# Two hybrid blocks on one core: low parts of block 1's input weights by an accumulating transfer

## The chip, the cores and the metric

One core of one Trainium2 chip runs the whole program in one launch. The metric is the device time in microseconds (us), the median of several runs. All profiles here are of that one core.

## What is computed

Two models stand one behind the other, each with two layers on 512 tokens of width 1024. Block 1 prepends 16 meta tokens, so it works on T1 = 528 columns. A layer of it is, cut to what matters here:

```python
hn = rms_norm(h, norm_mix_g[l])
proj = hn @ w_in[l]                     # 1024 x 2560
q, k, v, xr, gate = jnp.split(proj, splits, axis=-1)
# q, k: rms_norm, partial rope, differential attention with v
# xr: causal conv, two gates, linear recurrence, times gelu(gate)
h = h + jnp.concatenate([o_attn, o_rec], axis=-1) @ w_out[l]
h = h + (silu(g) * u) @ w_down[l]       # g, u = rms_norm(h) @ w_gu[l]
```

Block 2 (another mixer, cross attention to a memory, a squared-relu MLP) follows; the change does not touch its work.

## The kernel before

**Products from two parts.** All large products run on TensorE (PE) in the fp32r format. Each fp32 weight and each activation is split into a high part (the value rounded to fp32r) and a low part (the rest), and a product is three passes: high x high (L589), low weight x high activation (L592), high weight x low activation (L595). `dense` issues these for one 128x128 tile of weights and 528 columns in two halves of 264; `token_major` (L684, L686, L688) does the same for the value projection `w_v`.

**Pieces.** Weights come in pieces of 128 x 1024 fp32 (512 KB), in one long order over the whole program. In each layer of block 1 the order is 4 pieces of `w_v`, 16 pieces of `w_in` (k, q, xr and gate tiles), 8 of `w_out`, then the feed-forward. SyncE's queue (SP) loads piece n into one of 3 staging buffers (`load`, L2654). ScalarE (ACT) copies it to the high half of one of 3 `weights_hi_lo` buffers (`split_hi`, L1196) once TensorE has finished piece n-3. VectorE (DVE) subtracts the high part from the staged weights and writes the low half (`split_lo`, L1766). SP may refill a staging buffer when both have read it.

**Steps of block 1's attention stage.** Every engine runs the same 80 steps, written out by hand, each in its own program order. Four steps are one tile of `w_in`: step s works on tile t = s // 4 with two of its eight 128-row chunks. Tiles alternate between two PSUM slots, and VectorE evicts a tile at s % 4 == 3 (L2013). ScalarE splits the high part of tile t+2 at the end of its step s = 4t, VectorE the low part near the end of its step 4t+1. So 14 of the 16 pieces are split inside steps 0, 4, ..., 52; the first two are split before the steps, behind the third and fourth piece of `w_v`. Between the tiles' products the steps hold small work that goes from engine to engine: attention units at fixed steps (PE scores L778 and L782, DVE maxima L1907 to L1910, ACT exponentials L1278, DVE reciprocals L1888, POOL scaling L2534, DVE combination L1991, PE transposes L848 and L851, ACT copies L1332 to L1338, PE weighted sums L860 and L864), norms of q and k and the rope (PE sums L661, DVE L1915, ACT L1238, L1240 and L1286, DVE L1787 to L1789, L1921, L1926), and the gates of the recurrence (DVE convolution L1934, PE L661, ACT tanh L1300, ACT L1306 to L1310, POOL L2547 to L2554, DVE scan L1949). Step 2 of layer 0 has a chain of small VectorE instructions (L1816 to L1845) that begins with two small ScalarE exponentials (L1433, L1435). ScalarE loads a table (1.28 us) whenever the function changes to one of another table.

**Queues.** POOL (GpSimd) issues no transfer in the kernel before: loads and stores go by SP's queue, a few by ScalarE's. Waits are on semaphores, and every engine works through its own queue in order.

Durations of single instructions stand in the rows below. The lines that the diff touches are in `split_hi`, `split_lo`, `pool_attention`, `sync_program`'s `load`, and `Kernel.low`:

```python
w.wait_ge(*K.done("hi", n))                                  # split_lo, VectorE
e.tensor_tensor(lo[:, 0:cols], K.staged(n)[:, 0:cols], hi[:, 0:cols].bitcast(F32), ALU.subtract)
```

Of the kernel before, what the change touches and what calls it, by code (L numbers as in the profile page):

```python
# [12 lines left out]
ALU = mybir.AluOpType  # L13
ACT = mybir.ActivationFunctionType
# [5 lines left out]
DEPTH = 2  # L20
# [38 lines left out]
STAGING, PARTS, TEMPS = 3, 3, 16  # L59
# [2 lines left out]
WARM = 16  # L62

LINE = 1024 // 4
LINE_PAD = 32
ACT_COLS = -(-DC * T1 // LINE) * LINE


# [15 lines left out]
def columns(params):  # L84
# [25 lines left out]
    root_act=("qk_root_act", "sub_root_act", "rec_root_act", "ln_root_act"),  # L110
    var=("qk_var", "sub_var", "rec_var", "ln_var"), square=("qk_square", "sub_square", "rec_square", "ln_square"),
    norm_stat=("qk_stat", "sub_stat", "rec_stat", "sq_stat", "mean_sum", "shift_sum"),
    hid_hi=("hid_hi2", "gx_hi", "gx_columns_hi"), hid_lo=("hid_lo2", "gx_lo", "gx_columns_lo"),
).items() for name in names}


class Tally:
# [14 lines left out]
    def did(self, name, *key, by=1):  # L132
        sem = SEM_OF.get(name, name)
        self.value[sem] = self.value.get(sem, 0) + by
        if self.sems is None:
            assert (name, key) not in self.at, (name, key)
        self.at[name, key] = self.value[sem]
        return self.sem(name), by

    def done(self, name, *key):  # L140
        return self.sem(name), self.at[name, key] if self.sems is not None else 0
# [17 lines left out]
class Counted:  # L159
# [5 lines left out]
    def wait_ge(self, sem, value):  # L165
        return self

    def dma_start(self, out, src):
        return self

    def matmul(self, out, weights, moving, start=True, stop=True):
# [55 lines left out]
def along(row, width):  # L227
    if width <= BANK:
# [6 lines left out]
ORDER1 = [("xr", 0), ("k", 0), ("q", 0), ("k", 1), ("xr", 1), ("q", 1), ("k", 2), ("q", 2), ("xr", 2), ("g", 0),  # L235
          ("k", 3), ("q", 3), ("xr", 3), ("g", 1), ("g", 2), ("g", 3)]
AT1 = {tile: n for n, tile in enumerate(ORDER1)}
W_IN = {"q": 0, "k": HEADS, "xr": 2 * HEADS, "g": 3 * HEADS}
# [67 lines left out]
PIECES = pieces()  # L306
PIECE = {key: n for n, key in enumerate(PIECES)}
# [91 lines left out]


POOL_SPLIT = {s: 4 + (s - TOK_STEPS) // 4 + 2 for s in range(IDX_STEP + 9, MEM_STEP, 8)}
POOL_PIECES = {PIECE["w_tok", _l, 0] + ahead for _l in range(DEPTH) for ahead in POOL_SPLIT.values()}


class Kernel:
# [57 lines left out]
        return ap[:, 0, :], ap[:, 1, :]  # L463

    def low(self, n):
        return self.done("lo_pool" if n in POOL_PIECES else "lo", n)

    def piece(self, n):
        name, *at = PIECES[n]
        ap = self.t[name]  # L470
        if name in ("w_down", "w_ff2"):
            l, m, k0, k1 = at
            return ap[l, m, :, k0 * P:k1 * P]
        return ap[tuple(at)]
# [715 lines left out]
def split_hi(e, w, K, n):  # L1190
    if n < len(PIECES):
        w.wait_ge(*K.done(LANDED[n % STAGING], n))
        if n >= PARTS:
            w.wait_ge(*K.done("product", n - PARTS))
        cols = K.piece(n).shape[-1]
        e.activation(K.parts(n)[0][:, 0:cols], K.staged(n)[:, 0:cols], ACT.Copy).then_inc(*K.did("hi", n))  # L1196


def scalar_start(e, w, K):
# [43 lines left out]
def scalar_attention(e, w, K, l):  # L1243
    m, did, done = K.m, K.did, K.done
    first = PIECE["w_v", l, 0]
    for p in range(3):
        split_hi(e, w, K, first + p + 3)
# [510 lines left out]
        scalar_block2(e, w, K, l)  # L1758


def split_lo(e, w, K, n, name="lo"):
    if n < len(PIECES):
        cols = K.piece(n).shape[-1]
        hi, lo = K.parts(n)
        w.wait_ge(*K.done("hi", n))
        e.tensor_tensor(lo[:, 0:cols], K.staged(n)[:, 0:cols], hi[:, 0:cols].bitcast(F32), ALU.subtract).then_inc(  # L1766
            *K.did(name, n))
# [371 lines left out]
def vector_mixers(e, w, K, l):  # L2139
# [4 lines left out]
    for s in range(TOK_STEPS, STEPS2 + 2):  # L2144
# [89 lines left out]
        if s == MEM_STEP:  # L2234
            for n in range(DC // 2):
# [3 lines left out]
                                ALU.subtract).then_inc(*did("in_lo", "mem", l, n))  # L2239
        if s % 4 == 1 and TOK_STEPS + 4 < s <= MEM_STEP + 1 and s not in POOL_SPLIT:  # L2240
            split_lo(e, w, K, first + 4 + (s - TOK_STEPS) // 4 + 2)
# [4 lines left out]
def vector_normed(e, w, K, l, name, key, alpha, early=False):  # L2246
# [57 lines left out]
    for n in range(half + 1):  # L2304
        low(n)
# [207 lines left out]
def square_sums(e, w, K, stage, l, width):  # L2513

    total = K.xc[:, 0:width]
    for k in range(1, DC):
        w.wait_ge(*K.done("square", stage, l, k))
        if k > 1:
            w.wait_ge(*K.done("square_sum", stage, l, k - 1))
        square = K.g1 if k == DC - 1 else K.sq1[k % 3]  # L2520
        e.tensor_tensor(total, total, square[:, 0:width], ALU.add).then_inc(*K.did("square_sum", stage, l, k))  # L2521


def pool_attention(e, w, K, l):
    m, did, done = K.m, K.did, K.done
    w.wait_ge(*done("landed_rope"))
    for s in range(STEPS1):
        if s - 2 in UNIT_AT1[l]:
            u, h, i = UNIT_AT1[l][s - 2]
            q0, rows, keys, whole = unit1(i)  # L2530
            b = K.probs1[u % 2][1][0:rows, 0:keys]
            w.wait_ge(*done("rates", l, u))
            w.wait_ge(*done("small", l, "done"))
            e.tensor_scalar(b, b, m["small"][u % 4][0:rows, 7:8], m["lam"][0:rows, l, 5:6], ALU.mult, ALU.mult).then_inc(  # L2534
                *did("scaled1", l, u))
        if s - 3 in STAT_AT1:
            kind, n = STAT_AT1[s - 3]
            dst = (K.k if kind == "k" else K.q)[:, n, :]
            w.wait_ge(*done("normed", l, kind, n))
            e.tensor_tensor(dst, K.raw1[kind == "q"], m["rope"][:, 0, :], ALU.mult).then_inc(*did("cos", l, kind, n))  # L2540
        for n in range(REC_TILES):
            r = GATE1[n, 0]
            if s == r + 1:
                half_rate = m["lsig"][:, l, n:n + 1]
                w.wait_ge(*done("gate_tanh", l, n, 0))
                w.wait_ge(*done("small", l, "done"))
                e.tensor_scalar(K.tr, K.tr, half_rate, half_rate, ALU.mult, ALU.add).then_inc(*did("rate", l, n))  # L2547
            if s == r + 3:
                w.wait_ge(*done("half_tanh", l, n))
                e.tensor_scalar(K.tr, K.tr, 0.0, None, ALU.max).then_inc(*did("max", l, n))  # L2550
            if s == r + 5:
                w.wait_ge(*done("mult_first", l, n))
                w.wait_ge(*done("gated_in", l, n))
                e.tensor_tensor(K.xc, K.xc, K.tr, ALU.mult).then_inc(*did("scan_in", l, n))  # L2554
        if s == SUBROOT[1] + 3:
            mixed1_lo(e, w, K, l, 1, K.q[:, 1, :], "in_lo_pool")
        if s - 1 in RECSQ:
            n = RECSQ.index(s - 1)
            if 0 < n < REC_TILES - 1:
                w.wait_ge(*done("rec_square", l, n))  # L2560
                if n > 1:
                    w.wait_ge(*done("rec_sums", l, n - 1))
                e.tensor_tensor(K.xc, K.xc, (K.xc, K.tr, K.ti)[n], ALU.add).then_inc(*did("rec_sums", l, n))
    square_sums(e, w, K, "f", l, T1 if l + 1 < DEPTH else T2)


def pool_mixers(e, w, K, l):
    m, did, done = K.m, K.did, K.done
    for s in range(TOK_STEPS, STEPS2):
        if s - 2 in UNIT_AT2:  # L2570
# [3 lines left out]
            e.tensor_scalar(prob, prob, m["small"][u % 4][:, 7:8], None, ALU.mult).then_inc(*did("scaled", l, u, 1))  # L2574
        if s in POOL_SPLIT:
            split_lo(e, w, K, PIECE["w_tok", l, 0] + POOL_SPLIT[s], "lo_pool")
        if s in ROT_AT2:
# [67 lines left out]
def sync_program(e, K):  # L2645
    w = Waits(e)
    m, t, did, done = K.m, K.t, K.did, K.done

    def load(n):
        if n >= STAGING:  # L2650
            w.wait_ge(*done("hi", n - STAGING))
            w.wait_ge(*K.low(n - STAGING))
        src = K.piece(n)
        e.dma_start(K.staged(n)[:, 0:src.shape[-1]], src).then_inc(*did(LANDED[n % STAGING], n, by=16))  # L2654

    for c in range(DC):
        e.dma_start(m["x"][:, c, META:T1], t["x_t"][:, c]).then_inc(*did(f"landed_x{c}", by=16))
        if c in (0, 2, 4):
            load(c // 2)
    e.dma_start(K.lams[:, 0:DEPTH * 4 * HEAD_DIM], t["lambdas"]).then_inc(*did("landed_lams", by=16))  # L2660
    e.dma_start(m["consts"][:, :], t["consts"][:, 0:C_CAUSAL]).then_inc(*did("landed_consts", by=16))
    e.dma_start(K.gates, t["w_gates"][0]).then_inc(*did("landed_gates", 0, by=16))
    e.dma_start(m["rope"][:, 0:2, :], t["consts"][:, C_COS1:C_COLS].rearrange("p (a n) -> p a n", a=2)).then_inc(
        *did("landed_rope", by=16))
    e.dma_start(K.once[:, 0:2 * P], t["consts"][:, C_CAUSAL:C_COS1]).then_inc(*did("landed_once", by=16))
    e.dma_start(m["par2"][:, :, :], t["params2"]).then_inc(*did("landed_params2", by=16))
    for n in range(STAGING, len(PIECES)):
        load(n)
    for c in range(DC):
        w.wait_ge(*done("ln_out", "w_ff2", DEPTH - 1, c))  # L2670
        e.dma_start(K.out[:, c, :], m["x"][:, c, META:T1]).then_inc(*did("stored", c, by=16))
    w.wait_ge(*K.last("stored"))
# [6 lines left out]
def build(nc, t, out):  # L2679
    with ExitStack() as ctx:  # L2680
        def sb(name, cols, dt=F32):
            return ctx.enter_context(nc.sbuf_tensor(name, [P] + list(cols), dt))

        sb("to_line", [LINE_PAD])
        m = dict(
# [197 lines left out]
```

## Time and profile before

| | us |
|---|---|
| median of 3 runs | 2858.15 |
| lowest and highest run | 2857.96, 2858.54 |
| span of the profiled execution | 2853.0 |
| busy in it: PE, weight loads of PE | 2772.6, 2353.1 |
| busy in it: DVE, ACT, POOL | 1639.5, 1267.9, 403.3 |

The span is counted from the first to the last instruction of the profiled execution; no separate whole time is given for that execution. The median of the runs is 5.15 us above the span, which is start and end around the instructions. "Busy" of PE counts overlapped matmuls with modelled ends, so short waits below some 0.2 us are hidden in it; the row of the weight load (PEld) beside a matmul then still shows them. In the rows, "<-" behind a time names what ended the idle time of the engine before that instruction.

### The profile page before, as it was taken

How to read it: one execution, taken by the hardware profiler on the slowest of the kernel's cores; microseconds unless marked ns; L12 is line 12 of the kernel's file. 1: busy time of each engine (PE TensorE's matmuls, PEld its weight loads, DVE VectorE, ACT ScalarE, POOL GpSimd, SP SyncE). 2: the span in 40 equal slices, each digit the busy share in tenths (PEclk: the TensorE clock that was granted, in tenths of full speed). 3: DMA queues.
4: the chain of work that ended last, by engine and by line, in shares of the span. 5: the costliest groups of instructions: out<-in, count | busy, mean ns of one | idle time of the engine just before them, and what ended most of it. 6: DMA issues, size and time to landing. Idle time of an engine off the chain costs nothing.

```text
span 2853.0 us, 39111 instructions
## 1 busy us (share of the span) xinstructions
PE 2772.6 (97%) x15784; PEld 2353.1 (82%) x15784; DVE 1639.5 (57%) x2465; ACT 1267.9 (44%) x2133; POOL 403.3 (14%) x305
## 2 busy tenths in 40 slices
PE   9999999999989999999999999999999999999997
PEld 8878999999877788887668888888776688888886
DVE  6776545454777745454876466333658764753335
ACT  5674322224674422233564545333445644443333
POOL 2222000001222000001333120000313331200003
PEclk9999999999999999999999999999999999999999
DMA  4112232232112233332123223333222232233322
GB/s 153 45 45 67 89 97 85 94 92 83 49 45 74 93 96 97 102 93 89 56 75 126 88 67 96 98 95 96 85 82 63 75 126 81 67 104 96 96 96 67
DMA packets 71923, 244.35 MB, mean 86 GB/s; under 512 B 9153, under 2 KB 10817, under 8 KB 71745
## 3 DMA queue, kind: packets, MB, share of 16 engines
q1 hardware_dynamic: 67392, 237.28, 26.4%
q10 hardware_dynamic: 4352, 4.58, 0.5%
q8 instruction: 126, 2.06, 0.3%
q14 instruction: 53, 0.43, 0.0%
HBM read 239.73 MB, written 2.10 MB: 85 GB/s over the span
## 4 chain that ended last, share of the span: by engine, by line
PE 86%; DVE 8%; ACT 4%; issue 2%; POOL 0%; DMA 0%; ACTq 0%; DVEq 0%; SPq 0%
PE psum L589 24%; PE psum L595 24%; PE psum L592 24%; PE psum L661 2%; PE psum L684 1%; PE psum L688 1%; PE psum L686 1%; PE psum L922 1%; PE psum L1095 1%; PE psum L1107 1%; PE psum L950 1%; PE psum L939 1%; PE psum L975 1%; DVE weights_hi_lo L1766 1%; PE psum L778 1%
## 5 line engine op out<-in xcount | busy, mean ns | idle before, releaser
L589 PE MATMUL psum<-act_hi_lo,weights_hi_lo 128*128 128x264 f32 (+2 forms) x2544 | 777.6, 345 | 3.7 <-ACT temp L1300 2.8
L592 PE MATMUL psum<-act_hi_lo,weights_hi_lo 128*128 128x264 f32 (+2 forms) x2544 | 752.2, 335 | 1.9 <-DVE weights_hi_lo L1766 1.9
L595 PE MATMUL psum<-act_hi_lo,weights_hi_lo 128*128 128x264 f32 (+2 forms) x2544 | 753.4, 335 | 0.0
L1196 ACT ACTIVATE weights_hi_lo<-weights_float 128x1024 fp32r<-128x1024 f32 (+2 forms) x446 | 463.6, 1042 | 499.8 <-PE psum L595 430.6
L1766 DVE TENSOR_TENSOR weights_hi_lo<-weights_float,weights_hi_lo 128x1024 fp32r<-128x1024 f32 (+2 forms) x432 | 540.7, 1252 | 219.0 <-ACT weights_hi_lo L1196 217.8
L589 PE MATMUL psum<-hidden_hi_lo,weights_hi_lo 128*128 128x512 f32 (+2 forms) x1584 | 520.2, 358 | 3.7 <-DVE x_residual L2020 1.4
L595 PE MATMUL psum<-hidden_hi_lo,weights_hi_lo 128*128 128x512 f32 (+2 forms) x1584 | 512.2, 353 | 1.4 <-DVE hidden_hi_lo L2030 1.4
L592 PE MATMUL psum<-hidden_hi_lo,weights_hi_lo 128*128 128x512 f32 (+2 forms) x1584 | 511.8, 353 | 1.3 <-DVE weights_hi_lo L1766 1.3
L589 PEld LDWEIGHTS psum<-act_hi_lo,weights_hi_lo 128*128 128x128 f32 x2544 | 440.5, 189 | 68.1 <-issue 17.7
L595 PEld LDWEIGHTS psum<-act_hi_lo,weights_hi_lo 128*128 128x128 f32 x2544 | 439.3, 189 | 47.9
L592 PEld LDWEIGHTS psum<-act_hi_lo,weights_hi_lo 128*128 128x128 f32 x2544 | 438.7, 189 | 47.7 <-issue 2.6
L589 PEld LDWEIGHTS psum<-hidden_hi_lo,weights_hi_lo 128*128 128x128 f32 x1584 | 280.1, 189 | 44.9 <-DVE x_residual L2020 2.0
L595 PEld LDWEIGHTS psum<-hidden_hi_lo,weights_hi_lo 128*128 128x128 f32 x1584 | 279.8, 189 | 42.3 <-DVE hidden_hi_lo L2030 2.0
L592 PEld LDWEIGHTS psum<-hidden_hi_lo,weights_hi_lo 128*128 128x128 f32 x1584 | 279.7, 189 | 40.4 <-DVE weights_hi_lo L1766 1.7
L2036 DVE SCALAR_TENSOR_TENSOR x_residual<-x_residual,psum 128x512 f32<-128x512 f32 (+1 forms) x108 | 74.7, 691 | 275.2 <-PE psum L595 275.2
L2436 DVE TENSOR_TENSOR hidden_hi_lo<-temp,hidden_hi_lo 128x512 fp32r<-128x512 f32 x52 | 36.0, 692 | 172.2 <-ACT hidden_hi_lo L1697 172.2
L1409 ACT ACTIVATE hidden_hi_lo<-temp 128x528 fp32r<-128x528 f32 (+1 forms) x44 | 28.1, 639 | 201.8 <-DVE temp L2072 201.8
L2605 POOL TENSOR_TENSOR act_hi_lo<-x_residual 128x512 fp32r<-128x512 f32 x4 | 8.9, 2221 | 736.7 <-DVE x_residual L2036 736.7
L2521 POOL TENSOR_TENSOR temp<-temp 128x528 f32<-128x528 f32 (+1 forms) x28 | 43.6, 1558 | 479.7 <-ACT temp L1232 479.0
L1726 ACT ACTIVATE temp<-psum 128x512 f32<-128x512 f32 x52 | 31.1, 598 | 136.5 <-PE psum L595 136.5
L1404 ACT ACTIVATE temp<-temp 128x528 f32<-128x528 f32 (+1 forms) x44 | 28.1, 639 | 132.9 <-DVE temp L2060 132.8
L2574 POOL TENSOR_SCALAR temp<-temp,small 128x512 f32<-128x512 f32 (+3 forms) x48 | 54.8, 1143 | 186.3 <-DVE small L2157 186.1
(294 smaller groups left out, 3343.0 us busy)
## 6 DMA issues: line engine op xcount, KB each, us to landing
weights_float<-in_w_ff SPq DMA_DIRECT2D x128, 512.0 KB, 3.6
weights_float<-in_w_gu SPq DMA_DIRECT2D x88, 512.0 KB, 3.6
weights_float<-in_w_in SPq DMA_DIRECT2D x70, 512.0 KB, 3.7
weights_float<-in_w_down SPq DMA_DIRECT2D x32, 448.0 KB, 3.3
weights_float<-in_w_out SPq DMA_DIRECT2D x16, 512.0 KB, 3.6
weights_float<-in_w_down SPq DMA_DIRECT2D x16, 512.0 KB, 3.5
weights_float<-in_w_mv SPq DMA_DIRECT2D x16, 512.0 KB, 3.3
weights_float<-in_w_mix SPq DMA_DIRECT2D x16, 512.0 KB, 3.5
```

The costliest lines, as they stand in the source:

```text
L589: e.matmul(slot[:, place:place + c1 - c0], w_hi[:, col], x_hi[:, c0:c1], start=first, stop=False)
L592: e.matmul(slot[:, place:place + c1 - c0], w_lo[:, col], x_hi[:, c0:c1], start=False, stop=False)
L595: mm = e.matmul(slot[:, place:place + c1 - c0], w_hi[:, col], x_lo[:, c0:c1], start=False, stop=final)
L661: mm = e.matmul(slot[:, place:place + c1 - c0], weights, moving[:, c0:c1], start=first, stop=final)
L684: e.matmul(bank, act[:, 0, here], w_hi[:, wk], start=k == 0, stop=False)
L1196: e.activation(K.parts(n)[0][:, 0:cols], K.staged(n)[:, 0:cols], ACT.Copy).then_inc(*K.did("hi", n))
L1726: e.activation(raised(f), K.bank[2 * RING["w_ff1", l, f]], ACT.Relu).then_inc(*did("relu", l, f))
L1766: e.tensor_tensor(lo[:, 0:cols], K.staged(n)[:, 0:cols], hi[:, 0:cols].bitcast(F32), ALU.subtract).then_inc(*K.did(name, n))
L2036: e.scalar_tensor_tensor(along(x, width), along(x, width), alpha, across(K.psum[slot], width), ALU.mult, ALU.add).then_inc(*K.did(*mark))
L2436: e.tensor_tensor(lo, raised(f), hi.bitcast(F32), ALU.subtract).then_inc(*did("hid_lo2", l, f))
L2521: e.tensor_tensor(total, total, square[:, 0:width], ALU.add).then_inc(*K.did("square_sum", stage, l, k))
L2574: e.tensor_scalar(prob, prob, m["small"][u % 4][:, 7:8], None, ALU.mult).then_inc(*did("scaled", l, u, 1))
```

## The change

For the 16 pieces of `w_in` of each of block 1's two layers (32 pieces in all) ScalarE writes, right after the high part, the negated weights in fp32r, which is the negated high part, into the low half of the buffer. POOL's queue then issues a transfer of the same piece from memory with the operation "add" onto that low half, which leaves weights minus high part there. VectorE's subtraction of these pieces is gone, and TensorE waits for the transfer in its place. SP waits for the negation in place of the low part before it refills a staging buffer. POOL issues the first two transfers before its step 0 and the others at the end of its steps 1, 5, ..., 53. Some semaphores are shared by names that one engine signals in order, a scratch area for POOL's transfers grows from 256 to 1024 bytes, and a padding tensor grows with it so that later tensors keep their place within a line.

```diff
 LINE = 1024 // 4
-LINE_PAD = 32
+LINE_PAD = 96
@@
+    bias=("far", "near"), lam_exp=("lsig_exp",), mean=("mean_square",), conv_first=("conv2_first",), cube=("gelu_tanh",),
+    hi=("negated",),
@@
+SUM_PIECES = {PIECE["w_in", _l, _n] for _l in range(DEPTH) for _n in range(16)}
+SUM_LOW = [f"lo_sum{n}" for n in range(PARTS)]
@@
     def low(self, n):
+        if n in SUM_PIECES:
+            return self.done(SUM_LOW[n % PARTS], n)
         return self.done("lo_pool" if n in POOL_PIECES else "lo", n)
+
+    def read(self, n):
+        return self.done("negated", n) if n in SUM_PIECES else self.low(n)
@@ split_hi
         e.activation(K.parts(n)[0][:, 0:cols], K.staged(n)[:, 0:cols], ACT.Copy).then_inc(*K.did("hi", n))
+        if n in SUM_PIECES:
+            e.activation(K.parts(n)[1][:, 0:cols], K.staged(n)[:, 0:cols], ACT.Copy, scale=-1.0).then_inc(*K.did("negated", n))
@@
+def add_low(e, w, K, n):
+    w.wait_ge(*K.done("negated", n))
+    e.dma_start(K.parts(n)[1], K.piece(n), accum_op=ALU.add).then_inc(*K.did(SUM_LOW[n % PARTS], n, by=16))
@@ split_lo
-    if n < len(PIECES):
+    if n < len(PIECES) and n not in SUM_PIECES:
@@ pool_attention
+    first = PIECE["w_in", l, W_IN[ORDER1[0][0]] + ORDER1[0][1]]
     w.wait_ge(*done("landed_rope"))
+    for p in range(2):
+        add_low(e, w, K, first + p)
     for s in range(STEPS1):
...
+        if s % 4 == 1 and s // 4 + 2 < len(ORDER1):
+            add_low(e, w, K, first + s // 4 + 2)
@@ load
-            w.wait_ge(*K.low(n - STAGING))
+            w.wait_ge(*K.read(n - STAGING))
@@ kernel
-    nc = bacc.Bacc("TRN2", ..., dynamic_dma_scratch_size=256)
+    nc = bacc.Bacc("TRN2", ..., dynamic_dma_scratch_size=1024)
```

## Rows read from the trace of the kernel before

**Rows 1.** The page: busy us, share of the span and instructions of each engine.

```profile
PE 2772.6 (97%) x15784; PEld 2353.1 (82%) x15784; DVE 1639.5 (57%) x2465; ACT 1267.9 (44%) x2133; POOL 403.3 (14%) x305
```

**Rows 2.** Windows: stretch, length, busy PE, PEld, DVE, ACT, POOL; clock, DMA share, GB/s.

```profile
35.00:175.00 140.00, 129.73 (x941) 115.92 (x940) 101.28 (x179) 90.46 (x161) 32.59 (x29) 0.99 0.16 50
...
250.00:640.00 390.00, 389.11 (x3190) 388.58 (x3189) 193.21 (x253) 106.45 (x133) 10.85 (x7) 1.00 0.29 90
...
690.00:830.00 140.00, 128.45 (x954) 116.01 (x952) 99.92 (x151) 91.83 (x156) 32.23 (x29) 1.00 0.16 50
```

**Rows 3.** Waits of PE, 35 to 185 us: us in total, times, longest.

```profile
PE psum L778 <- ACT arena L1278: 2.4, 2, 1.7
PE psum L778 <- DVE arena L2013: 1.6, 1, 1.6
PE psum L661 <- ACT temp L1286: 1.5, 2, 0.8
PE psum L851 <- DVE arena L1991: 1.2, 1, 1.2
```

**Rows 4.** Lines L1766 and L1196 in layer 0's steps: ns min/median/max.

```profile
L1766 DVE TENSOR_TENSOR weights_hi_lo<-weights_float,weights_hi_lo x14: 1201/1218/1226, 38.7 to 183.9; 128x1024 fp32r<-128x1024 f32 x14
...
L1196 ACT ACTIVATE weights_hi_lo<-weights_float x14: 1039/1044/1063, 37.5 to 180.1; 128x1024 fp32r<-128x1024 f32 x14
```

**Rows 5.** Timeline, layer 0 from step 0: start, us, engine, [idle before <- releaser].

```profile
37.51 1.06 ACT L1196 ACTIVATE weights_hi_lo<-weights_float 128x1024 fp32r<-128x1024 f32 x1 [2.06 <-PE psum L688]
...
40.12 0.16 DVE L1816 TENSOR_TENSOR lambdas<-lambdas 128x1 f32<-128x1 f32 x1 [0.22 <-ACT lambdas L1433]
...
48.85 0.19 PEld L661 LDWEIGHTS psum<-temp,arena 128*128 128x128 f32 x1 [0.27 <-issue]
```

**Rows 6.** Timeline, layer 1 at step 20 to 22.

```profile
733.73 1.04 ACT L1196 ACTIVATE weights_hi_lo<-weights_float 128x1024 fp32r<-128x1024 f32 x1
...
736.78 0.69 ACT L1278 ACTIVATE arena<-psum,small 128x528 f32<-128x528 f32 x1
...
737.61 0.52 PEld L661 LDWEIGHTS psum<-temp,consts 128*128 128x128 f32 x3 [0.20 <-ACT arena L1278]
```

**Rows 7.** Timeline, layer 0 behind step 28, and layer 1's counterpart.

```profile
104.72 1.05 ACT L1196 ACTIVATE weights_hi_lo<-weights_float 128x1024 fp32r<-128x1024 f32 x1
...
113.42 0.46 PE L860 MATMUL psum<-temp,arena 128*128 128x128 f32 x2 [0.16 <-ACT temp L1338]
...
763.40 0.39 ACT L1338 ACTIVATE temp<-psum 128x256 f32<-128x256 f32 x1 [0.30 <-PE psum L851]
```

**Rows 8.** Timeline, layer 0 behind steps 40 and 44.

```profile
143.53 1.04 ACT L1196 ACTIVATE weights_hi_lo<-weights_float 128x1024 fp32r<-128x1024 f32 x1
...
146.63 1.16 PE L661 MATMUL psum<-temp,arena 128*128 128x264 f32 x4 [1.05 <-ACT temp L1300]
...
154.24 1.04 ACT L1196 ACTIVATE weights_hi_lo<-weights_float 128x1024 fp32r<-128x1024 f32 x1
...
156.52 1.26 PE L778 MATMUL psum<-arena 64*128 64x512 f32 x8 [0.76 <-ACT arena L1278]
```

**Rows 9.** Timeline, layer 0: ACT behind the split of step 36.

```profile
134.07 0.49 ACT L1338 ACTIVATE arena<-psum 128x384 f32<-128x384 f32 x1 [2.29 <-PE psum L851]
```

**Rows 10.** The page: DMA queue 1, and issues of `w_in` pieces with us to landing.

```profile
q1 hardware_dynamic: 67392, 237.28, 26.4%
...
weights_float<-in_w_in SPq DMA_DIRECT2D x70, 512.0 KB, 3.7
```

**Rows 11.** Timeline: layer 1's splits of `w_in` 0 and 2, and SP's `w_in` loads.

```profile
675.10 1.06 ACT L1196 ACTIVATE weights_hi_lo<-weights_float 128x1024 fp32r<-128x1024 f32 x1 [5.86 <-PE psum L688]
...
689.82 1.06 ACT L1196 ACTIVATE weights_hi_lo<-weights_float 128x1024 fp32r<-128x1024 f32 x1 [2.06 <-PE psum L688]
...
12.75 134.97 SPq L2654 DMA_DIRECT2D weights_float<-in_w_in  x16
```

**Rows 12.** Timeline, POOL behind step 29 in layer 0.

```profile
108.70 0.46 POOL L2534 TENSOR_SCALAR arena<-arena,small,lambdas 128x144 f32<-128x144 f32 x1 [3.74 <-DVE small L1888]
```

More of the change, by code:

```diff
@@ L166, in wait_ge, with dma_start @@
         return self
-    def dma_start(self, out, src):
+    def dma_start(self, out, src, accum_op=None):
         return self
@@ L2872 @@
     arrays = layout({name: np.asarray(a) for name, a in inputs.items()})
-    nc = bacc.Bacc("TRN2", target_bir_lowering=False, num_devices=1, dynamic_dma_scratch_size=256)
+    nc = bacc.Bacc("TRN2", target_bir_lowering=False, num_devices=1, dynamic_dma_scratch_size=1024)
     feed, aps = {}, {}
```

## The prediction

> **What bounds the kernel.** I read the page's busy times first: PE is busy 2772.6 of 2853.0 us [rows 1], so all other engines together can give back at most 80.4 us, and only where PE waits. The windows say where that is. In the feed-forward stretch from 250 to 640 us PE lacks 0.9 us of 390. In the steps of block 1's attention it lacks 140 - 129.73 = 10.3 us in layer 0 and 140 - 128.45 = 11.5 us in layer 1, with VectorE busy 72% and ScalarE 65% [rows 2]. These are the stretches in which the 32 pieces are split. No engine is full there; what counts is which wait of PE ends last, and on whom. The waits say that ScalarE releases as many of them as VectorE: exponentials and squares against evictions and combinations [rows 3], and the gate tanh [rows 8]. Nobody waits there for the subtraction itself. So the question of this change is not how much work VectorE loses, but in which uninterrupted queue run of which engine the removed and the added instruction stand when PE is waiting for something behind them.
>
> **Removed: VectorE's subtraction.** 32 x 1.22 us [rows 4] = 39 us of VectorE time. It is worth something only where PE's releaser stands behind it in one run without idle time. I followed each of PE's waits back. The eviction (1.6 us) [rows 3] and the norms' waits hang on runs of VectorE that begin, behind the subtraction, with idle time that PE or ScalarE ends. L1926 at steps 33 and 53 follows the subtraction without a gap, but PE's rope product ends within 0.05 us of its start. The combinations (L1991) wait for POOL or for a ScalarE root. I find no wait of PE with a subtraction in the run ahead of it, so I take 0; the bounds are 0 and, if every wait on VectorE shrank, what rival C prices.
>
> **Added: ScalarE's negation.** The same form as the high copy, so 1.04 us each [rows 4], 32 x 1.04 = 33 us of ScalarE time. Most of it falls into idle time: behind step 36 for example ScalarE next sat idle 2.29 us until PE [rows 9]. Where a releaser of PE stands in the same run behind the copy, PE starts 1.04 us later, and as PE is the full engine nothing later takes that back. The places, each read off the timeline:
> - Layer 0, step 0: the copy at 37.51 us is followed by the small exponentials that start VectorE's small chain, on which VectorE sat idle 0.22 us. The chain delays the first eviction, the convolution and so the first gate product, whose weight load at 48.85 us had already waited 0.27 us [rows 5]: 1.04. Layer 1 has no such chain.
> - Step 20, both layers: the copy, a table load and two exponentials follow without a gap; the second ends 0.14 us before PE's rope sum, which had waited for it 0.20 us [rows 6]: 2 x 1.04.
> - Step 28, layer 0: a full run from 104.72 us to the copy of turned probabilities, for which PE waited at 113.42 us: 1.04. In layer 1 the same copy had been idle 0.30 us and PE came 1.3 us later [rows 7]: 0.
> - Step 40, both layers: the gate tanh right behind the copy, for which PE already waits 1.05 us: 2 x 1.04.
> - Step 44, both layers: the exponentials right behind the copy, for which PE waits 0.76 us at 156.52 us [rows 8]: 2 x 1.04. The wait after it hangs on the same run and is no second loss.
> Together 8 x 1.04 = 8.3 us. The other 20 negations in the steps and the four before them I cost at nothing: the idle time of ScalarE behind them hides them, and if it were gone each would cost up to 1.04 us more. That is the upper bound of this term, 33 us; the lower one is 0.
>
> **Moved: who makes the low part.** PE's wait moves from VectorE to a transfer that POOL issues. The tightest piece is `w_in` 0: its high copy starts at 675.10 us in layer 1 and its product when `w_v` 3 ends, just before 689.82 us [rows 11]. Copy and negation take 2.1, which leaves 12.6 us; the later tiles leave about as much or more, since they are two tiles ahead too. No row shows an accumulating transfer. The nearest is the plain load of the same bytes, 3.7 us to landing; all of queue 1's packets took 26.4% of 2853 us for 237.28 MB, which is 1.7 us for 0.52 MB [rows 10]. The other end is a transfer several times as slow, which I put at 20 us, above all that the windows allow. I take one whose moving part doubles: 3.7 + 1.7 = 5.4 us, well inside 12.6, so 0 for PE. The Trainium skill says in "Collectives: The Full Stack" (The bandwidth ceiling) that a reduce runs at about half the rate of a copy because the add needs two source reads; by it the landing would be this same 5.4 us, and no run here shows it yet.
>
> POOL: 16 issues a layer behind its steps' work. Each wait for a negation stands ahead of POOL's next step. The tightest of these places is behind step 29: the next instruction comes at 108.70 us after 3.74 us idle, of which the negation (to 106.8) leaves 1.9 [rows 12]. I take up to 1.9 us for one on POOL and so 0; with 4 us it would push L2534 and a combination at two or three steps a layer, some 1 us each, 2 to 6 in all. The memory traffic rises by 32 x 0.52 = 16.8 MB, in stretches that move 50 GB/s [rows 2]: 0. SP's refill condition comes earlier, and no load is waited for: 0. The shared semaphores keep the order of one engine: 0. The larger scratch and pad keep the tensors' places: 0.
>
> **Sum.** The profiled execution had a span of 2853.0 us, 5.15 below the median of the runs. 2853.0 + 8.3 = 2861.3 us of span, and 2858.15 + 8.3 = **2866.5 us**. A measurement of this kernel tells about 0.2%, 5.7 us, from no change.
>
> **The rivals.**
> - A, the delay is absorbed: PE's later waits shrink by what the earlier ones lost, because some releasers run on their own clock (a combination of VectorE that waits for POOL). Then half or less remains, 0 to 5.7 us: about 2861. For it: rows 3 has such a wait of 1.2 us. Against it: nearly every run of ScalarE and VectorE here begins with a release by PE.
> - B, the transfer is late. It decides from a landing of 12.6 us. A pair of tiles takes 2 x 135 / 15 = 18 us [rows 11], and copy, negation and landing must fit in it: at 20 us landing each pair is 4.1 us too long, 7 pairs in 2 layers, +57 us, 2915; at 14 to 16 us only the first, shorter tiles stall, +10 to +20. Against it: the plain load has three times the room that it needs. For it: POOL's path and the add are not in the trace. The Trainium skill warns in "SBUF — State Buffer" (SBUF: two separate sides) that VectorE's two-port operations lock GpSimd out while it writes descriptors, and gives 620 ns that became 3100. By that ratio a plain landing of 3.7 would be 18.5 us, on this rival's side; it needs such an operation standing over each issue, and the VectorE rows here are mostly two-input operations and copies of 0.3 us. I give the lock 0.04 of this rival's 0.15.
> - C, faster: VectorE's queue, 0.9 of its 1.2 us shorter each tile, reaches PE through evictions and combinations, and ScalarE's negation disappears in idle time. PE's two largest groups of waits on VectorE in layer 0 are 1.6 and 1.2 us [rows 3]; twice that for layer 1 is 5.6, and with the smaller waits I estimate at most 10: 2848. It decides if subtractions do stand in the runs that release PE; I found none.
> - D, the low part is made as said but costs POOL 4 us an issue: +2 to +6 on top, 2870. It lies inside my range.
>
> **How the numbers follow.** The forecast, alone or with D: 0.56; A: 0.21; B: 0.15; C: 0.08. Below 2852.4 us is only C: 0.08. Within 0.2% are A and the low edge of the forecast (five or fewer of the eight places hold): 0.21 + 0.03 = 0.24. Slower are the rest of the forecast and B: 0.68. The range takes in A almost whole from 2859.5 us and goes up through D, up to half of the unseen extra places, and B's mild part, to 2884 us; it leaves out C, A's edge and B's late end.
>
> **What would show it.** ScalarE's busy time +33 us and VectorE's -39; PE's idle time in the two stretches up by 5.2 in layer 0 and 3.1 in layer 1. The wait at 146.6 us becomes 2.1 us, the one at 156.5 us 1.8, and the rope sum behind step 20 shows a wait of 1.2 us on L1278. PE's waits on the transfer are nil, and its landing is under 12 us. I am wrong if PE's L592 waits for the transfer, if POOL's issue takes over 2 us and L1991's waits grow, or if those five places show no longer waits.

## The result, and the profile after

The changed kernel takes 2863.85 us (median of 10 runs, 2862.35 to 2867.32), the kernel before on the same chip 2857.37 us (10 runs, 2856.12 to 2859.88). The ratio is 1.0025, 95% interval 1.0016 to 1.0034: slower by 7.1 us (4.6 to 9.7). The forecast was slower by 8.3 us, 2866.5 us, with a range of 2859.5 to 2884.

Busy times, queues and transfers on the page of the changed kernel (to be set against [rows 1], [rows 4] and [rows 10]; a DMA line ends with KB each and the us from issue to landing):

```profile
PE 2778.2 (97%) x15784; PEld 2356.6 (82%) x15784; DVE 1602.7 (56%) x2433; ACT 1298.3 (45%) x2165; POOL 428.9 (15%) x337
...
q1 hardware_dynamic: 67392, 237.28, 25.9%
q0 software_dynamic: 4608, 16.78, 3.5%
...
weights_float<-in_w_in SPq DMA_DIRECT2D x70, 512.0 KB, 3.8
weights_hi_lo<-in_w_in POOLq DMA_DIRECT2D x32, 512.0 KB, 7.9
```

VectorE lost 36.8 us of work, ScalarE gained 30.4, POOL 25.6, and 16.78 MB of transfers came on. The span rose by 8.6 us, to 2861.6. None of the work that moved has that size; the waits of PE tell where the time went.

The timeline of the changed kernel at the places named in the prediction (start us, duration us, engine, line; L1205 is the high copy, L1207 the negation, L670 and L787 are PE's L661 and L778 of before). First steps 0, 20 and 28 of layer 0:

```profile
38.01 1.06 ACT L1205 ACTIVATE weights_hi_lo<-weights_float 128x1024 fp32r<-128x1024 f32 x1 [2.06 <-PE psum L697]
38.98 1.04 ACT L1207 ACTIVATE weights_hi_lo<-weights_float 128x1024 fp32r<-128x1024 f32 x1
...
50.40 0.46 PE L670 MATMUL psum<-temp,arena 128*128 128x264 f32 x1 [1.10 <-issue]
...
88.09 1.16 PE L670 MATMUL psum<-temp,consts 128*128 128x264 f32 x4 [0.94 <-ACT arena L1289]
...
110.11 0.22 PE L787 MATMUL psum<-arena 64*16 64x16 f32 x4 [0.27 <-ACT arena L1289]
...
116.88 0.46 PE L869 MATMUL psum<-temp,arena 128*128 128x128 f32 x2 [0.76 <-ACT temp L1349]
...
121.66 0.18 PE L860 MATMUL psum<-consts,arena 16*16 16x16 f32 x1 [0.59 <-DVE arena L2009]
```

Then steps 40 and 44, in layer 0 and (from 804 us) in layer 1, where the kernel before waited 1.52 and 1.19 us, as the second block shows:

```profile
146.39 1.04 ACT L1205 ACTIVATE weights_hi_lo<-weights_float 128x1024 fp32r<-128x1024 f32 x1
147.34 1.04 ACT L1207 ACTIVATE weights_hi_lo<-weights_float 128x1024 fp32r<-128x1024 f32 x1
...
150.45 1.16 PE L670 MATMUL psum<-temp,arena 128*128 128x264 f32 x4 [1.99 <-ACT temp L1311]
...
161.28 1.26 PE L787 MATMUL psum<-arena 64*128 64x512 f32 x8 [1.71 <-ACT arena L1289]
...
804.71 1.69 PE L670 MATMUL psum<-temp,arena 128*128 128x264 f32 x3 [2.47 <-ACT temp L1311]
...
816.31 1.26 PE L787 MATMUL psum<-arena 64*128 64x512 f32 x8 [1.94 <-ACT arena L1289]
```

```profile
797.88 1.16 PE L661 MATMUL psum<-temp,arena 128*128 128x264 f32 x4 [1.52 <-ACT temp L1300]
...
807.57 1.26 PE L778 MATMUL psum<-arena 64*128 64x512 f32 x8 [1.19 <-ACT arena L1278]
```

What the reader is to see: in layer 0 the copy and the negation each last 1.04 us, but start 0.95 apart, so a negation delays what is behind it by 0.95. The waits of 1.05 and 0.76 us [rows 8] became 1.99 and 1.71; the rope sum behind step 20, whose weight load had waited 0.20 (layer 1's is in [rows 6], layer 0's is as long), waits 0.94; the 0.16 at step 28 [rows 7] is 0.76, with 0.27 ahead of it.

I laid the same instructions of both traces beside each other and read how far PE's start had moved. The kernel with the negation on VectorE (run e7 below) serves as the reference: its median is that of the kernel before, and it has no half-clock stretch (one in which PE's granted clock is 0.5, 1.2 GHz) near 164 us, which before has. The move grows by 1.01 at step 0, 0.95 at step 20, 0.34 and 0.59 at step 28, falls by 0.61 right behind it, where PE's wait for a combination shrank (above: 0.59 us at 121.66 us, 1.19 before), and grows by 0.93 at step 40 and 0.94 at step 44. That is +4.2 us for layer 0. In layer 1 half-clock stretches lie near the same places in this pair of profiles (3.4 us each from 739.4, 804.2 and 817.9 us in the changed kernel's), so single steps can't all be read off there. The traces of e9 (below) and of before have no such stretch at these three places: set beside each other, PE's start moves by 0.95, 0.93 and 0.95 at steps 20, 40 and 44. That is 2.8 us, and a gate product ahead of them, behind a gate tanh of ScalarE, adds 0.3 (also in e3, below, and not in e2). Sum: 7.3 us, against the ratio's 7.1.

### The profile page after: what moved, and what is told of

The parts are those of the page before. It is cut to its first block, busy times and chain, and to the rows that moved or that the text cites. A ratio compares the mean times of both kernels' runs of the same rounds, so it can differ in the third digit from the quotient of the medians.

```text
span 2861.6 us, 39138 instructions
## 1 busy us (share of the span) xinstructions
PE 2778.2 (97%) x15784; PEld 2356.6 (82%) x15784; DVE 1602.7 (56%) x2433; ACT 1298.3 (45%) x2165; POOL 428.9 (15%) x337
## 3 DMA queue, kind: packets, MB, share of 16 engines
q0 software_dynamic: 4608, 16.78, 3.5%
## 4 chain that ended last, share of the span: by engine, by line
PE 85%; DVE 9%; ACT 4%; issue 2%; POOL 0%; DMA 0%; ACTq 0%; DVEq 0%; SPq 0%
PE psum L598 24%; PE psum L601 23%; PE psum L604 23%; PE psum L670 2%; PE psum L693 1%; PE psum L697 1%; PE psum L695 1%; PE psum L931 1%; PE psum L1104 1%; PE psum L1116 1%; PE psum L959 1%; PE psum L948 1%; PE psum L984 1%; ACT weights_hi_lo L1205 1%; DVE weights_hi_lo L1784 1%
## 5 line engine op out<-in xcount | busy, mean ns | idle before, releaser
L1205 ACT ACTIVATE weights_hi_lo<-weights_float 128x1024 fp32r<-128x1024 f32 (+2 forms) x446 | 463.7, 1042 | 498.7 <-PE psum L604 431.0
L1784 DVE TENSOR_TENSOR weights_hi_lo<-weights_float,weights_hi_lo 128x1024 fp32r<-128x1024 f32 (+2 forms) x400 | 501.6, 1255 | 201.5 <-ACT weights_hi_lo L1205 200.2
L2605 POOL TENSOR_TENSOR arena<-temp,rope_tables 128x512 f32<-128x512 f32 x14 | 18.1, 1291 | 441.2 <-ACT temp L1488 441.2
```

## Experiments

The ratio is that of each kernel to the kernel before on the same chip; "us" is (ratio - 1) x 2857. Kernels whose computation differs: e2, whose transfers add the weights to what the low half held.

| run | what is different | ratio (95%) | us |
|---|---|---|---|
| the change | | 1.0025 (1.0016 to 1.0034) | +7.1 |
| e1 | negations without the transfers | 1.0020 (1.0010 to 1.0029) | +5.7 |
| e2 | transfers without the negations | 1.0001 (0.9993 to 1.0010) | +0.3 |
| e3 | 24 pieces, without the eight places | 0.9996 (0.9987 to 1.0004) | -1.1 |
| e4 | the eight places alone | 1.0023 (1.0014 to 1.0032) | +6.6 |
| e5 | 29 pieces, five negations moved | 0.9998 (0.9989 to 1.0006) | -0.6 |
| e6, e11 | before, three splits a layer moved | 0.9996 (0.9987 to 1.0005), 0.9994 (0.9985 to 1.0003) | -1.1, -1.7 |
| e7 | VectorE negates | 1.0001 (0.9992 to 1.0010) | +0.3 |
| e8 | transfers two steps later | 1.0024 (1.0016 to 1.0033) | +6.9 |
| e9 | transfers four steps later | 1.0036 (1.0021 to 1.0051) | +10.3 |
| e10 | every negation twice | 1.0094 (1.0079 to 1.0110) | +26.9 |
| e12 | e6 with one subtraction later | 0.9991 (0.9982 to 1.0000) | -2.6 |

### Which part costs: e1 and e2

```diff
 split_lo (e1; the transfers are gone)
-    if n < len(PIECES) and n not in SUM_PIECES:
+    if n < len(PIECES):
...
-        w.wait_ge(*K.done("hi", n))
+        w.wait_ge(*K.done("negated" if n in SUM_PIECES else "hi", n))
```

> The changed kernel with the transfers taken out: ScalarE's 32 negations stay, and VectorE subtracts as before, over them. Theory S (the whole cost is ScalarE's negation in eight places, 0.95 us each as the profile after shows, 7.6 in all, less 0.6 absorbed): +7 us against the kernel before, about 2864.5 where that one has 2857.4, and the waits of 1.7 to 2.0 us at 150 and 161 us. Theory T (the transfers or POOL's issues cost it): 0, waits of 0.8 and 1.0 there. Theory V (the removed subtractions give back some us, and the negations cost more than 7): +10 or more.

```diff
 read, split_hi, add_low (e2)
-        return self.done("negated", n) if n in SUM_PIECES else self.low(n)
+        return self.done("hi", n) if n in SUM_PIECES else self.low(n)
...
-        if n in SUM_PIECES:
-            e.activation(K.parts(n)[1][:, 0:cols], K.staged(n)[:, 0:cols], ACT.Copy, scale=-1.0).then_inc(*K.did("negated", n))
...
-    w.wait_ge(*K.done("negated", n))
+    w.wait_ge(*K.done("hi", n))
```

> The changed kernel without ScalarE's negations: POOL's transfer adds the weights to what the low half held, as soon as the high copy is there, so the low parts of these 32 pieces have wrong values; VectorE's subtractions are gone. Theory S: 0 us against before (2857.4), within 1.5. Theory T: +7. Theory V: -3 or less. Landing 7.9 us and POOL's issue 0.9 us as in the profile after, in every theory.

e1 has nearly the whole cost (+5.7), e2 none (+0.3). e2 by itself shows a sum: 32 subtractions fewer and 32 transfers more come to nothing, within 2.9 us. That neither hides the other is told by the waits: those of PE for VectorE from 35 to 190 us are in e2 what they are in before (1.6, 1.2, 0.9, 0.5 and 0.4 us), and there is none for a transfer. So the subtractions are worth nothing, and the transfers cost nothing. e1's waits are those of the whole change. Its waits of PE from 35 to 190 us (us in total, times, longest), and under them e2's:

```profile
PE psum L785 <- ACT arena L1287: 3.7, 3, 1.7
PE psum L668 <- ACT temp L1309: 2.0, 1, 2.0
...
PE psum L668 <- issue: 1.0, 1, 1.0
PE psum L668 <- ACT arena L1287: 0.9, 1, 0.9
```

```profile
PE psum L670 <- ACT temp L1309: 1.1, 1, 1.1
...
PE psum L670 <- issue: 0.2, 1, 0.2
```

In e2 the step-40 wait is 1.1 again, and of the waits at steps 0 and 20 only 0.2 us are left ("issue"). Its profiled span was 2859.4 us, though: that execution took 2861.24 us, the longest of its eleven, 5.1 above their median. The waits of one profile say more here than its length.

### Which places: e3 and e4

```diff
-SUM_PIECES = {PIECE["w_in", _l, _n] for _l in range(DEPTH) for _n in range(16)}
+AT_STEPS = [{0, 20, 28, 40, 44}, {20, 40, 44}]
+SUM_PIECES = {PIECE["w_in", _l, 0 + W_IN[ORDER1[_s // 4 + 2][0]] + ORDER1[_s // 4 + 2][1]]
+              for _l in range(DEPTH) for _s in range(-8, 56, 4) if _s not in AT_STEPS[_l]}   # e3
+              for _l in range(DEPTH) for _s in AT_STEPS[_l]}                                 # e4
...
 add_low
+    if n not in SUM_PIECES:
+        return
```

> The change for 24 of the 32 pieces: the eight whose negation stands ahead of a releaser of PE (layer 0: steps 0, 20, 28, 40, 44; layer 1: steps 20, 40, 44) are split as before. Theory S: 0 to +0.5 us against before (0.2 to 0.3 for a gate tanh behind a table load in layer 1). Theory T: 24/32 of the cost, +5. A theory that the delay is spread over all negations: +5 as well.

> The change for those eight pieces alone. Theory S: +6.5 to +7.6 us against before, nearly all of what the whole change costs. Theory T and the theory of a spread delay: 8/32 of it, +2.

24 of the 32 pieces change nothing that can be told (-1.1 us, interval -3.7 to +1.1), eight pieces make nearly all of it (+6.6). The busy times do not show this: e3 gave ScalarE three quarters of the added work. The busy times on e3's page, then on e4's:

```profile
PE 2772.5 (97%) x15784; PEld 2350.8 (82%) x15784; DVE 1611.0 (56%) x2441; ACT 1289.9 (45%) x2157; POOL 422.4 (15%) x329
```

```profile
PE 2777.6 (97%) x15784; PEld 2356.2 (82%) x15784; DVE 1630.9 (57%) x2457; ACT 1275.6 (45%) x2141; POOL 409.0 (14%) x313
```

ScalarE is busier by 22 us in e3 (span 2851.7) and by 8 us in e4 (span 2861.1).

### The same work in another place: e5 and e7

```diff
+MOVED = [{0: 1, 20: 22, 40: 43}, {20: 22, 40: 43}]        # e5; steps 28 (layer 0) and 44 split as before
...
 scalar_attention, end of step s
+        for step, at in MOVED[l].items():
+            if s == at:
+                negate(e, w, K, first + 4 + step // 4 + 2)
```

> The change for 29 of the 32 pieces, with five negations moved off the places that release PE: that of step 0 in layer 0 behind the small exponentials, that of step 20 to the end of step 22 and that of step 40 to the end of step 43 in both layers, where ScalarE sat idle. The pieces of step 28 in layer 0 and of step 44 in both layers are split as before. Theory S (a negation costs by its place): 0 against the kernel before, within 1 us. Theory T (transfers or POOL cost): +6. A theory that the number of negations counts: 29/32 of the change's cost, +6. A late landing (negation of step 40 ends about 10 us ahead of its tile, landing 7.9): PE waits of under 1 us at L601 of the changed kernel.

```diff
 split_lo on VectorE (e7), in place of ScalarE's L1207
-    if n < len(PIECES) and n not in SUM_PIECES:
+    if n in SUM_PIECES:
+        w.wait_ge(*K.done("hi", n))
+        e.tensor_scalar(K.parts(n)[1], K.staged(n)[:, :], -1.0, None, ALU.mult).then_inc(*K.did("negated", n))
+    elif n < len(PIECES):
...
```

> The change with the negation on VectorE, where the subtraction stood, and not on ScalarE. Theory S: 0 against the kernel before, within 1.5 us, since no wait of PE stands behind that place of VectorE's queue, and ScalarE works as before. Theory T: +7. The negation takes 0.6 to 1.2 us on VectorE.

Both are at zero. e5's timeline at step 20: the exponentials come first, and the negation at 85.29 us stands in idle time of ScalarE; at step 40 the wait is 1.05 us, as before:

```profile
85.20 0.20 ACT L1297 ACTIVATION_READ_ACCUMULATOR arena<-psum,small 128x1 f32 x1
85.29 1.05 ACT L1215 ACTIVATE weights_hi_lo<-weights_float 128x1024 fp32r<-128x1024 f32 x1
...
85.46 1.16 PE L674 MATMUL psum<-temp,consts 128*128 128x264 f32 x4
...
146.51 1.16 PE L674 MATMUL psum<-temp,arena 128*128 128x264 f32 x4 [1.05 <-ACT temp L1319]
```

e7's lines for the subtraction that is left and for the negation (duration in ns, least, median, most):

```profile
L1784 DVE TENSOR_TENSOR weights_hi_lo<-weights_float,weights_hi_lo x400: 1091/1225/2367, 7.4 to 2820.4; 128x1024 fp32r<-128x1024 f32 x121, 128x896 fp32r<-128x896 f32 x11, 128x912 fp32r<-128x912 f32 x2
L1779 DVE TENSOR_SCALAR weights_hi_lo<-weights_float x32: 671/685/694, 26.8 to 833.7; 128x1024 fp32r<-128x1024 f32 x32
```

VectorE negates in 0.69 us what ScalarE negates in 1.04, in a place that no wait of PE hangs on: PE's waits from 35 to 190 us are those of before. It is the version to choose if the transfers are wanted, and it wins nothing either.

### The room of the transfer: e8 and e9

```diff
-        if s % 4 == 1 and s // 4 + 2 < len(ORDER1):
-            add_low(e, w, K, first + s // 4 + 2)
+        if s % 4 == 3 and s // 4 + 2 < len(ORDER1):               # e8
+            add_low(e, w, K, first + s // 4 + 2)
+        if s % 4 == 1 and s >= 4 and s // 4 + 1 < len(ORDER1):    # e9
+            add_low(e, w, K, first + s // 4 + 1)
```

> The changed kernel with POOL's transfers of the steps issued two steps later (about 4.5 us). My account (landing 7.9 us, and 8 steps of 2.2 to 3.2 us from a copy to its tile, less four for issue): they land 0 to 2 us ahead of their tiles, PE waits for them under 1 us in all, and the time is that of the changed kernel, +7 against before. If the landing is less even than its 5.8 to 8.4 us, or POOL comes late behind its own waits: L601 of PE waits for transfers, +10 to +20.

> The changed kernel with POOL's transfers of the steps issued four steps later, at the end of the second step of the tile ahead. What is left to a landing of 5.7 to 7.9 us is then about the 2.7 steps to the tile, 6 us and more where a step has other work. My account: PE now waits for transfers in about half of its 28 tiles, 1 to 4 us each, the time rises by 20 to 80 us over the changed kernel, and L601 and its weight load show it: so the room is real, and between two and four steps of delay it ends. If the transfer had more room than I worked out: no wait, +7 against before as with two steps.

e8 costs nothing more (+6.9 against +7.1), and PE waits for no transfer. In e9 it does. Two waits of layer 0 in its timeline, and from the view of the transfer's line who waited for it in the whole run (us, times):

```profile
64.56 0.51 PE L601 MATMUL psum<-act_hi_lo,weights_hi_lo 128*128 128x264 f32 x2 [3.14 <-DMA weights_hi_lo<-in_w_in]
...
73.10 0.51 PE L601 MATMUL psum<-act_hi_lo,weights_hi_lo 128*128 128x264 f32 x2 [0.65 <-DMA weights_hi_lo<-in_w_in]
```

```profile
  PE psum L601: 9.0, 7
```

So the room ends between two and four steps, as worked out, but my size for it was wrong: seven waits and not half of 28, 9.0 us of waiting, and the medians are 3.2 us apart, against the 20 to 80 I expected. (e9 has three executions, and the profiled one is the longest of them, 3.8 us above their median, so the 9.0 and the 3.2 are not of one execution.) The two longest waits, 3.14 us here and 3.12 in layer 1, are early, where a step holds little besides the tile; in the later, longer steps most transfers had landed. Part of this waiting comes back: up to the eviction wait at 83.87 us the two waits shown, 3.8 us, move PE by 1.7 us only, since four waits behind them shrink, those of 0.70, 0.44 and 0.78 us to nothing and that of 1.58 [rows 3] to 1.34. So a delay of PE by a transfer is in part taken back here, which the delay of ScalarE at the eight places is not: the waits that shrink are those for squares of ScalarE and for VectorE's statistics and eviction, which these two waits of PE held up less than PE itself.

### More of it: e10

```diff
-    hi=("negated",),
+    hi=("negated", "negated_once"),
...
         if n in SUM_PIECES:
+            e.activation(K.parts(n)[1][:, 0:cols], K.staged(n)[:, 0:cols], ACT.Copy, scale=-1.0).then_inc(*K.did("negated_once", n))
+            w.wait_ge(*K.done("negated_once", n))
             e.activation(K.parts(n)[1][:, 0:cols], K.staged(n)[:, 0:cols], ACT.Copy, scale=-1.0).then_inc(*K.did("negated", n))
```

> The changed kernel with every negation done twice, the second after the first: ScalarE gets another 1.0 to 1.1 us at each place. Theory S: the same places pay again, 8 x 1.05 = 8.4 us, and some of the others join, since their idle time behind the negation is used up: +8 to +14 over the changed kernel, +15 to +21 against before. A theory of a fixed cost of the change (transfers, POOL's issues): +7 against before, as with one.

The second negation costs 19.8 us more, nearly three times the first, and above the range I had given. The old places paid another 1.1 each (3.08 us at step 40, 1.99 with one negation), and places whose cover one negation had just used up began to pay:

```profile
67.24 1.13 PE L670 MATMUL psum<-temp,consts 128*128 128x264 f32 x4 [1.69 <-ACT temp L1299]
...
107.80 1.16 PE L670 MATMUL psum<-temp,arena 128*128 128x264 f32 x4 [0.76 <-ACT temp L1313]
...
143.01 1.16 PE L670 MATMUL psum<-temp,consts 128*128 128x264 f32 x4 [0.73 <-ACT arena L1291]
...
159.13 1.27 PE L670 MATMUL psum<-temp,arena 128*128 128x264 f32 x4 [3.08 <-ACT temp L1313]
```

The first of these is one of two waits on the square behind an eviction: 1.5 us together before and with one negation [rows 3], 2.5 with two. The cost of one more microsecond on ScalarE is convex: all but zero in 24 places, but by little in many of them.

### A version that uses the reading: e6, e11, e12

If a negation costs 0.95 us in a place, the high copy that stands there already costs as much, as far as PE's wait reaches. e6 is the kernel before, with no part of the change, and three splits a layer moved:

```diff
+SPLIT_AT = {20: 22, 40: 43, 44: 47}
 scalar_attention; vector_attention the same with SPLIT_AT.get(step, step) + 1 and split_lo
-        if s % 4 == 0 and s < 4 * len(ORDER1):
-            split_hi(e, w, K, first + 4 + s // 4 + 2)
+        for step in range(0, 4 * len(ORDER1), 4):
+            if s == SPLIT_AT.get(step, step):
+                split_hi(e, w, K, first + 4 + step // 4 + 2)
```

> The kernel before, without any of the change, with the high copy and the subtraction of three pieces a layer moved to where ScalarE sat idle: those of step 20 to steps 22 and 23, of 40 to 43 and 44, of 44 to 47 and 48. Theory S says that in these places the high copy costs PE what the negation cost it, as far as PE's waits there reach: 2 x (0.2 at step 20 + 0.95 of the 1.05 at step 40 + 0.95 of the 0.76 and the wait behind it at step 44) = -4.2 us against before, 2853.2 where that one has 2857.4. If the waits only move to the next releaser (VectorE's combination, or the late subtraction): 0, or slower by up to 2.

> The kernel of the run with the moved splits once more, since its -1.3 us was inside the interval. Its profile showed about 1.4 us less a layer: the waits of 1.05 and 0.76 us on ScalarE are gone, but PE then waits 0.6 and 1.9 us for VectorE. Expected: -1 to -3 us against before, ratio 0.9990 to 0.9997; if the gain was chance, 0.

Less came than the 4.2 us: 1.1 and 1.7, both inside their intervals. The waits at steps 40 and 44 did go (the first wholly, the second from 0.76 to 0.57 us, now on VectorE), but two steps later stood one of 1.87 us that was not there before. VectorE, PE and POOL in e6 at that place:

```profile
165.25 1.73 DVE L1993 SCALAR_TENSOR_TENSOR arena<-arena,small 128x528 f32<-128x528 f32 x1 [0.38 <-POOL arena L2537]
166.90 1.21 DVE L1768 TENSOR_TENSOR weights_hi_lo<-weights_float,weights_hi_lo 128x1024 fp32r<-128x1024 f32 x1
168.04 0.28 DVE L1901 COPY arena<-psum 128x128 f32<-128x128 f32 x1
...
168.37 0.66 PE L849 MATMUL psum<-consts,arena 128*128 128x128 f32 x4 [1.87 <-DVE arena L1901]
...
165.10 1.31 POOL L2543 TENSOR_TENSOR arena<-temp,rope_tables 128x528 f32<-128x528 f32 x1
```

The subtraction that I had moved (L1768) stood right ahead of the copy that PE waited for. In this profile PE gains 1.9 us on before up to 163 us, and this one wait takes nearly all of it away; in layer 1 it is 2.0 gained and a wait of 1.76. So e6's own trace speaks for a gain near nothing. e12 puts the subtraction one step later (the cut is against e6):

```diff
+LOW_AT = {20: 23, 40: 44, 44: 49}
-            if s == SPLIT_AT.get(step, step) + 1:
+            if s == LOW_AT.get(step, step + 1):
```

> The moved splits, with the subtraction of step 44's piece one step later still, at step 49 in place of 48. In the profile of the moved splits that subtraction (1.21 us at 166.90 us) stood between the combination and the small copy at 168.04 us for which PE waited 1.87 us. If it gave back what the moved splits had won: -1.2 us a layer against them, so -2.4 us further, -3 to -5 us against the kernel before, ratio 0.9982 to 0.9990, and the wait of 1.87 us becomes about 0.7. If the combination itself, or POOL, sets that wait: no further gain, ratio 0.9995.

The wait fell from 1.87 to 0.72 us, as expected. Among e12's waits:

```profile
PE psum L850 <- DVE arena L1902: 0.7, 1, 0.7
```

The time is 2.6 us under the kernel before, with an interval that just reaches 1 (0.9982 to 1.0000): the only version here that is likely faster, and not by much. It is also less than the 3 to 5 us I had expected, and its lead over e6 and e11, 0.9 to 1.5 us, is inside their intervals. PE now waits for VectorE's combination there.

## Why the prediction was right, and where a size was off

**Bound and removed part: right.** PE's waits for VectorE are unchanged without the subtractions (e2), and subtractions gone and transfers added come to 0 within 2.9 us. Rival C falls with it.

**Added part: the eight places are right, each term 9% too large.** All eight pay, and no other but a gate tanh in layer 1 (0.3), which the prediction had at nothing. The term was sized by the duration of a copy, 1.04; ScalarE's instructions overlap, and the pitch, from one start to the next, is 0.95: 8 x 0.95 = 7.6 in place of 8.3. With the 0.3 added and the 0.6 that came back behind step 28 (next paragraph) that is the 7.3 of the moves; these two nearly cancel, which is luck and not reading. The trace of before already had the pitch: behind the copy at 154.24 us [rows 8] the next exponential starts 0.95 later.

```profile
155.19 0.57 ACT L1278 ACTIVATE arena<-psum,small 128x400 f32<-128x400 f32 x1
```

**Rival A: a small part of it is true.** Behind step 28 the move fell by 0.6, since the combination that PE waits for comes by a chain of its own. The prediction's sentence that nothing later takes a delay back was too strong for one of eight. At the other seven nothing came back. For a delay that does not pass through ScalarE the sentence fails more widely: in e9 over half of the first two waits came back.

**Transfer: the cover was right, the landing too low.** I took 5.4 us for the landing; it is 7.9 in the median. In e8, where the transfers are issued two steps after the load of the next piece and not with it, it is 5.6 in the same stretch. Queues of the changed kernel from 35 to 175 us (packets, MB, share of 16 engines), and the landings; in the second block e8's landing:

```profile
q0 software_dynamic: 1872, 6.82, 28.9%
q1 hardware_dynamic: 1784, 6.49, 15.7%
...
weights_hi_lo<-in_w_in POOLq DMA_DIRECT2D x13, 512.0 KB, 7.9
weights_float<-in_w_in SPq DMA_DIRECT2D x11, 512.0 KB, 4.1
```

```profile
weights_hi_lo<-in_w_in POOLq DMA_DIRECT2D x12, 512.0 KB, 5.6
```

Per byte the adding transfer holds the DMA engines (28.9 / 6.82) / (15.7 / 6.49) = 1.75 times as long as the load. The Trainium skill's page "Collectives: The Full Stack" (The bandwidth ceiling) puts a reduce at about half the rate of a copy for its ring collectives; this transfer is none, and the trace's 1.75 is near that factor. So the doubled moving part was well taken (e8's 5.6 against the 5.4), and what I left out is that the same negation also lets SP refill the staging buffer, so two transfers of 512 KB run at once. It changed nothing, because the room was 12.6 us by the prediction's estimate. Rival B decided from there, and e8 and e9 bracket its point. That rival's lock by VectorE is not seen: the landings lie between 5.8 and 8.4 us.

**POOL: right.** An issue takes 0.9 us, under the 1.9 that the tightest place leaves, so rival D falls too.

**What would show it.** ScalarE +30 (33 expected, again the pitch) and VectorE -37 (39). The waits were forecast at 2.1, 1.8 and 1.2, and are 1.99, 1.71 and 0.94 in layer 0. One sign was badly chosen: the idle time of PE in the two stretches. It rose by 2.7 and 0.2 us, not by 5.2 and 3.1, since a stretch of fixed times moves over the work and half-clock matmuls count as busy. The windows from 35 to 175 and 690 to 830 us after, against [rows 2]:

```profile
35.00:175.00 140.00, 127.06 (x917) 112.88 (x915) 85.36 (x163) 99.85 (x170) 42.54 (x42) 0.99 0.45 96
...
690.00:830.00 140.00, 128.28 (x904) 115.05 (x902) 81.24 (x130) 98.62 (x159) 41.17 (x40) 0.96 0.45 98
```

## What to carry to other kernels

Where one engine is full, price an instruction on another engine by what stands behind it in its queue until that engine next idles, not by the busy shares: here three quarters of the added work were all but free and one quarter cost nearly all. Use the start-to-start pitch, not the duration. And a cost of that kind has two sides: the instruction already standing in such a place can be moved out of it, but then look at what it is put in front of (e6 against e12).

## What the runs showed of the hardware that was not expected

**The clock of PE drops for 3 to 4 us at places that change from run to run.** From 164 to 168 us, in the same part of the work, before ran mostly at 1.2 GHz and e7 at 2.4 (columns: PE busy, granted clock, DMA share, GB/s); ahead of it PE had waited 1.7 us for ScalarE in both. First before, then e7:

```profile
164.00:168.00 4.00, 4.00 (x23) 0.57 0.00 0
```

```profile
164.00:168.00 4.00, 4.00 (x37) 1.00 0.19 37
```

PE starts 1.3 us later behind this stretch in before than in e7. Such a loss hides in the busy time, and it makes single profiles differ by more than the effect of one negation. What sets its place stays open.

**VectorE and POOL wait for each other on two-input operations.** VectorE's combination (528 columns) takes 1.73 us at 165.25 us in e6, where POOL's product runs from 165.10 to 166.41: until POOL ends, and 0.6 more. The same line takes 0.76 us where POOL is idle. It takes 0.77 where it starts first, by 0.08 us, and there POOL's product (1.32 us at 62.06 us) is the long one:

```profile
88.66 0.76 DVE L1993 SCALAR_TENSOR_TENSOR arena<-arena,small 128x528 f32<-128x528 f32 x1
...
199.93 0.77 DVE L1993 SCALAR_TENSOR_TENSOR arena<-arena,small 128x528 f32<-128x528 f32 x1
...
200.01 1.87 POOL L2557 TENSOR_TENSOR temp<-temp 128x528 f32<-128x528 f32 x1 [1.03 <-DVE temp L1948]
```

The Trainium skill describes this in "SBUF — State Buffer" (SBUF: two separate sides): a VectorE operation with two inputs from that memory and a GpSimd operation that reads it hold a port pair exclusively, and the second waits for the first to end. The trace agrees, in both orders and in both layers (1.73 us again at 813.74 us); the same combination is part of PE's last wait in e12, so POOL's product is the next thing to move there. That was not tried.
